# Differential attention: the two maps' score matmuls in turn, and each row maximum taken in two parts

## What is computed

```python
s = jnp.einsum('bqhmd,bkhmd->bhmqk', qi, k, preferred_element_type=jnp.float32) * scale
p = jax.nn.softmax(s, axis=-1)
pd = p[:, :, 0] - lam * p[:, :, 1]
return jnp.einsum('bhqk,bkhv->bqhv', pd.astype(v.dtype), v)
```

## Time and profile before

| what | value |
|---|---|
| median of 3 runs | 2270.38 us |
| runs | 2267.83 to 2270.40 us |
| span of the profiled execution | 2266.8 us |
| TensorE busy | 2191.9 us, 97% |
| VectorE busy | 1552.2 us, 68% |
| ScalarE busy | 815.4 us, 36% |
| instructions | 33980 |

### The profile page before, as it was taken

The page is one execution under the profiler, slowest core; times in us unless marked ns, Lnnn a source line. Parts: engine busy times, 40 slices in busy tenths (PEclk is TensorE's granted clock), DMA queues, the critical chain, the costliest instruction groups (busy, mean ns, idle before and its releaser), DMA issues.

```text
span 2266.8 us, 33980 instructions
## 1 busy us (share of the span) xinstructions
PE 2191.9 (97%) x13144; PEld 2105.5 (93%) x13144; DVE 1552.2 (68%) x2607; ACT 815.4 (36%) x1458; POOL 20.1 (1%) x31
## 2 busy tenths in 40 slices
PE   5999999999999999999999999999999999999997
PEld 4989999999999999889977779899999999999996
DVE  6977777778888776666668874686454556756556
ACT  5532222334111144654255662353232323421122
POOL 0000000000000000000000030000000000000000
PEclk9999999999999999999999999999999999999998
DMA  7433333344624304010110011132212123431312
GB/s 290 133 105 135 103 126 111 113 138 131 213 78 158 126 27 151 19 47 28 32 49 22 22 40 38 56 114 68 78 59 86 58 87 101 159 120 52 109 41 84
DMA packets 82292, 210.10 MB, mean 93 GB/s; under 512 B 9856, under 2 KB 36352, under 8 KB 82176
## 3 DMA queue, kind: packets, MB, share of 16 engines
q1 hardware_dynamic: 82176, 208.52, 27.4%
HBM read 172.56 MB, written 35.92 MB: 92 GB/s over the span
## 4 chain that ended last, share of the span: by engine, by line
PE 88%; DVE 7%; ACT 2%; DMA 1%; issue 1%; SPq 0%; DVEq 0%; ACTq 0%
PE ps L717 15%; PE ps L719 15%; PE ps L718 15%; PE ps L792 9%; PE ps L793 9%; PE ps L794 9%; PE ps L972 6%; PE ps L1043 4%; PE ps L1072 2%; PE ps L1058 1%; PE ps L954 1%; DVE sb_nmx L2286 1%; DVE sb_hL L1752 1%; DVE sb_tmp L1761 1%; PE ps L741 1%
## 5 line engine op out<-in xcount | busy, mean ns | idle before, releaser
L717 PE MATMUL ps<-sb_hH,sb_wH 128*128 128x384 f32 x1664 | 562.7, 338 | 10.2 <-DVE sb_hL L1752 4.7
L719 PE MATMUL ps<-sb_hH,sb_wL 128*128 128x384 f32 x1664 | 557.4, 335 | 0.0
L718 PE MATMUL ps<-sb_hL,sb_wH 128*128 128x384 f32 x1664 | 557.3, 335 | 0.0
L717 PEld LDWEIGHTS ps<-sb_hH,sb_wH 128*128 128x128 f32 x1664 | 313.4, 188 | 17.5 <-DVE sb_hL L1752 6.0
L718 PEld LDWEIGHTS ps<-sb_hL,sb_wH 128*128 128x128 f32 x1664 | 313.4, 188 | 1.1
L719 PEld LDWEIGHTS ps<-sb_hH,sb_wL 128*128 128x128 f32 x1664 | 313.4, 188 | 0.0
L2062 DVE SCALAR_TENSOR_TENSOR sb_x<-ps,sb_mod,sb_x 128x384 f32<-128x384 f32 (+2 forms) x384 | 186.2, 513 | 172.6 <-PE ps L719 167.2
L792 PE MATMUL ps<-sb_hH,sb_wH 128*128 128x384 f32 x704 | 236.1, 335 | 4.1 <-DVE sb_tmp L1922 3.9
L793 PE MATMUL ps<-sb_hL,sb_wH 128*128 128x384 f32 x704 | 235.9, 335 | 0.0
L794 PE MATMUL ps<-sb_hH,sb_wL 128*128 128x384 f32 x704 | 235.8, 335 | 0.0
L1226 ACT ACTIVATE sb_wH<-sb_wide 128x512 fp32r<-128x512 f32 x176 | 110.8, 633 | 229.1 <-DVE sb_wide L1806 224.0
(11 more groups left out here) (244 smaller groups left out, 3789.3 us busy)
## 6 DMA issues: line engine op xcount, KB each, us to landing
sb_raw<-in_w_gate SPq DMA_DIRECT2D x56, 512.0 KB, 3.7
sb_raw<-in_w_up SPq DMA_DIRECT2D x56, 512.0 KB, 3.6
sb_raw<-in_w_mod SPq DMA_DIRECT2D x56, 512.0 KB, 3.5
hidden<-sb_tmp SPq DMA_DIRECT2D x132, 192.0 KB, 2.2
sb_hid_raw<-hidden SPq DMA_DIRECT2D x40, 576.0 KB, 6.5
sb_raw<-in_w_dn SPq DMA_DIRECT2D x80, 256.0 KB, 2.7
sb_stage<-in_w_mod SPq DMA_DIRECT2D x4, 2048.0 KB, 15.4
sb_raw<-in_w_in SPq DMA_DIRECT2D x16, 512.0 KB, 3.5
```

What stands on the lines that cost most here:

```text
L717: pe.matmul(o, wH, xH, start=begin, stop=False)
L718: pe.matmul(o, wH, xL, start=False, stop=False)
L719: return pe.matmul(o, wL, xH, start=False, stop=end)
```

## The change

The six score matmuls of a full tile are issued strictly alternating between the maps. A new semaphore, `s_first`, is raised when the first 512 columns of a map are done. In a full tile VectorE takes four reductions, map 0 and map 1 over columns 0 to 511, then map 0 and map 1 over columns 512 to 1151, into a new small buffer `pmx`, waits for them, and takes the minimum of the two negated parts for both maps in one instruction, which raises `mx_ready` by two. Short tiles keep the two separate reductions. ScalarE's code is unchanged.

```diff
-PIECES = ((0, 0, 512), (0, 512, 1024), (1, 0, 512), (0, 1024, UNIT), (1, 512, 1024), (1, 1024, UNIT))
+PIECES = ((0, 0, 512), (1, 0, 512), (0, 512, 1024), (1, 512, 1024), (0, 1024, UNIT), (1, 1024, UNIT))
...
+def lat_before(u):
+
+    return u - u // QT - 1
...
+            pmx = sb("pmx", [P, 2, 2], F32, s)
...
+        s_first = sem("s_first")
...
                     if e == (UNIT if q else P):
                         mm.then_inc(s_ready, 1)
+                    elif b == 0:
+                        mm.then_inc(s_first, 1)
...
-            def maxima(u, m):
-
-                dve.wait_ge(s_ready, 2 * u + m + 1)
-                dve.tensor_reduce(nmx[:, u % 2, m:m + 1], unit(u, m), AX.X, ALU.max, negate=True).then_inc(mx_ready, 1)
+            def maxima(u):
+
+                nm = nmx[:, u % 2]
+                if u % QT == 0:
+                    for m in range(2):
+                        dve.wait_ge(s_ready, 2 * u + m + 1)
+                        dve.tensor_reduce(nm[:, m:m + 1], unit(u, m), AX.X, ALU.max, negate=True).then_inc(mx_ready, 1)
+                    return
+                for part, (b, e) in enumerate(((0, 512), (512, UNIT))):
+                    for m in range(2):
+                        if part == 0:
+                            dve.wait_ge(s_first, 2 * lat_before(u) + m + 1)
+                        else:
+                            dve.wait_ge(s_ready, 2 * u + m + 1)
+                        chain[0] += 1
+                        dve.tensor_reduce(pmx[:, part, m:m + 1], unit(u, m)[:, b:e], AX.X, ALU.max,
+                                          negate=True).then_inc(step, 1)
+                dve.wait_ge(step, chain[0])
+                dve.tensor_tensor(nm, pmx[:, 0], pmx[:, 1], ALU.min).then_inc(mx_ready, 2)
...
             for u in range(TILES + 3):
                 if u < TILES:
-                    for m in range(2):
-                        maxima(u, m)
+                    maxima(u)
```

## The result

| | before | after |
|---|---|---|
| median | 2270.39 us (4 runs) | 2292.40 us (4 runs) |
| lowest to highest | 2267.83 to 2270.52 | 2290.26 to 2293.65 |
| span of the profiled execution | 2266.8 | 2291.6 |
| granted clock, mean of the span | 0.992 | 0.988 |

The changed kernel is slower by a factor of 1.0097 (95% interval 1.0082 to 1.0111), 22 us. The forecast was 2281 with a range of 2273 to 2288: the direction holds, the size is twice what was forecast, and the time lies outside the range.

What follows compares the result with a forecast made beforehand. TensorE was taken as nearly full, with attention's repeating tile, through two nearly equal loops, setting the time. Tile 5.86 to 6.19, +0.33 over 32 full tiles, gives 10.6 us on 2270.4, about 2281, range 2273 to 2288.

Steps and rivals of the forecast that it cites:

- The sum for the maxima: VectorE's four parts and minimum: 2.98 us until ScalarE starts, giving a tile of 6.19 us against 5.86.
- The order of the scores: nothing: TensorE's score matmuls: both array halves already overlap fully, so alternating the maps neither gains nor slows map 0's chain.
- The wait in the queue bites: Rival, chance 0.17: map 1's wait in TensorE's queue delays map 0's second piece, 0.1 to 0.25 per tile, 2284 to 2289.
- M - S = 0.85: Load of map 1's first weights (M) after map 0's (S): about 0.85 us, where queue delay begins; nothing taken for it.
- Nothing for short tiles: Attention's short tile in each head keeps its old code, so no time was added for it.
- The clock: Granted TensorE clock: a TensorE that waits longer could see one more dip, about 3 us, added to the queue rival.
- early halves win: Rival, chance 0.05: first halves fill VectorE's 0.75 us wait, the copy comes earlier, tile 0.14 less, 2266.
- strict order brings a gain: Rival, chance 0.02: if matmuls start only in program order, map 1 could start earlier, at most 0.14 per tile, 2266.
- floor: Rival, chance 0.11: VectorE is early enough, tile 5.90 to 5.98 us, time 2272 to 2274.

Runs made afterwards that it cites:

- e2: Changed kernel with the scores' old order; only the maxima are split and joined: 2281.87 us, ratio 1.0061 to the kernel before.
- e5: Kernel before, whole maxima, scores reordered but map 0's third piece ahead of map 1's second: 2267.89 us, ratio 0.9997.
- e1: Kernel before with only the order of the six score matmuls changed to alternating, maxima whole: 2279.43 us, ratio 1.0046.
- e3: Changed kernel with map 0's third score piece issued ahead of map 1's second: 2281.59 us, ratio 1.0057 to the kernel before.
- e8: Kernel before with only the release changed, both whole maxima announced together after the second: 2291.15 us, ratio 1.0100.
- e4: Changed kernel with scores in old order, only map 0's maximum split, each map released by itself: 2264.49 us, ratio 0.9984 to the kernel before.
- e6: Changed kernel with two small minima instead of one, each releasing its own map: 2266.15 us, ratio 0.9999 to the kernel before.
- e7: Changed kernel with two small minima, each releasing its own map, and scores in the old order: 2267.29 us, ratio 0.9992.

## Why the prediction was right and wrong

- **The sum for the maxima** (2.98 from the first part to ScalarE, 6.19 per tile): right, as e2 shows with 6.18. Its terms: the 512-column part 0.68 (forecast 0.68), the two 640-column ones 1.56 together (0.74 + 0.82 = 1.56), the minimum 0.16 (0.16). So are its mechanism, that both maps are released together, and its rejection of the early halves as a gain in this form.
- **"The order of the scores: nothing"**: the step that failed. That a map's chain is not slowed by the other's is right, e5 is even with the kernel before. But the maxima don't wait for a piece to be done; they wait for its semaphore, and that comes in program order. The steady tile of before couldn't show it, since there no short piece stood behind a longer one of the other map that ended later. The third full tile of a head did (S + 2.44 instead of S + 2.24, above), and the rows of the prediction leave it out. The cost is 6.46 - 6.18 = 0.28 per tile in the changed kernel and 0.19 alone (e1). 32 x 0.28 = 9 us at most is most of the 11 that the forecast lacks; the rest is the clock and the short tiles. The rule that the prediction set aside, "TensorE: Matmul & The Clock Gate", The mechanism, in the Trainium skill, says strict FIFO in start and end. The starts of map 1 ahead of earlier passes of map 0 disagree with it; for the end, as far as a semaphore shows it, these runs agree. The prediction weighed only the starts.
- **"The wait in the queue bites"** was the slower rival, with 2284 to 2289. M did come 1.19 after S. But where e3 has that wait, M at 1.20, it loses nothing against e2: the picture of the rival was right and its price was not. The measured 2292 still lies above it.
- **M - S = 0.85 "just at the edge"**: it was 0.90 in e2 (0.85 forecast) and 1.19 in the changed kernel. The rule of the prediction, the tile less TensorE's own time from M to the next S, holds in both; that time is 5.27 instead of 5.34, and the tile was the term that was off.
- **Nothing for short tiles**: low by 0.3 us per head, about 1 us in all.
- **The clock**: named as an addition of about 3 us to a rival, not put in the sum. It took about 4 in attention in the profiled execution, and 2.4 behind it. In the steady stretch it fell in the three kernels e1, e8 and changed, and not in e2 and e3, whose tile is longer than e1's; what makes it fall is not settled by these runs. In the changed kernel TensorE waited several times in the few us before the dip at 1215, 0.36, 0.65 and 0.25 long; that this is the cause is only argued.
- **The low rivals** (early halves win, strict order brings a gain, floor) didn't come. The early halves do win once each map is released by itself: clearly in e4, and in the attention column of e6 and e7 too. TensorE's own tile is then 5.66, 0.20 under the 5.86 where the prediction had 0.14.

## What to carry to other kernels

When a chain alternates between two buffers, let each go by itself: joining two releases in one instruction saves an instruction and loses the head start of the first, here the whole difference between 5.86 and 6.40 us per tile. A maximum over a PSUM region can be begun on its first bank in time that is idle anyway, if the part behind the last matmul gets shorter and nothing else is put there. And before reordering matmuls on different halves of the array, ask whose semaphore stands behind which matmul in program order. Look at the tiles that are not steady, too: one of them showed this cost before anything was changed.

## What the runs showed of the hardware

- The semaphore of a matmul on one 64-row half of the array is raised only when the earlier ones in program order, on the other half, are done: map 0's last pass ended at 1239.02, VectorE, free by 1239.43, started at 1239.71, 0.06 after a pass of map 1 that ended at 1239.65; in the kernel before the same shows in the third full tile of a head (1255.98, 0.05 after 1255.93). Moving that one piece back brought 0.28 us per tile.
- The same two halves don't start in program order: before the change map 1's weights load 0.39 after S with four passes of map 0 ahead of them, and map 0 is none the slower.
- Reductions from PSUM took 0.281 us at 128 columns and 1.352 at 1152; the straight line through these gives 0.68 and 0.82 for 512 and 640, and 0.69 and 0.82 were measured.
- The clock cost time without any change of the work there: behind attention the same work took 912.4 us before and 914.7 in the changed kernel, where 12 us of it (1490 to 1502) ran at a granted clock of 0.72 instead of 1.00.
